# A two-layer retention and stick-breaking trunk: layers and retention loop written out, norm buffers moved to PSUM, and five smaller moves

## The reference

```python
for l in range(DEPTH):
    mod = c_act @ w_ada[l] + b_ada[l]
    shift1, scale1, gate1, shift2, scale2, gate2 = jnp.split(mod, N_MOD, axis=-1)
    h = _modulate(_rmsnorm(x, norm_mix_g[l]), shift1, scale1)
    x = x + gate1 * _mixer(h, w_in[l], w_ret_out[l], w_sb_out[l], w_mix_out[l])
    h2 = _modulate(_rmsnorm(x, norm_mlp_g[l]), shift2, scale2)
    u = jnp.square(jax.nn.relu(h2 @ w_up[l]))
    x = x + gate2 * (u @ w_down[l])
return _rmsnorm(x, final_g)
```

## Time and profile before

| | before |
|---|---|
| median of 3 runs | 2481.89 us (2480.94 to 2482.94) |
| the profiled execution: its time | 2484.95 us |
| its span | 2482.6 us |
| mean granted clock of TensorE | 0.98 |
| TensorE busy | 2403.6 us, 97% |
| GpSimd busy | 1126.0 us, 45% |
| VectorE busy | 1014.8 us, 41% |
| ScalarE busy | 893.6 us, 36% |
| read from HBM | 256.97 MB, 104 GB/s over the span |

### The profile page before, as it was taken

How to read it: one execution, slowest core, us unless ns; L and a number is a source line. 1 busy time by engine, 2 the same in 40 slices (tenths; PEclk the granted TensorE clock), 3 DMA queues, 4 the chain that set the end, 5 groups by cost and what they waited for, 6 DMA issues and landing times.

```text
span 2482.6 us, 33083 instructions
## 1 busy us (share of the span) xinstructions
PE 2403.6 (97%) x11946; PEld 1977.6 (80%) x11946; DVE 1014.8 (41%) x1521; ACT 893.6 (36%) x1005; POOL 1126.0 (45%) x1486
## 2 busy tenths in 40 slices
PE   6999999999999999999979999999999999999998
PEld 5787788788888878888858878878888787888886
DVE  6555455624442341221345564552444322321223
ACT  3222122245557332332322222222556753322332
POOL 2444434443334545554543444444433445455552
PEclk6999999999999999999989999999999999999999
DMA  6533536322222323323323534334222223233231
GB/s 221 166 125 101 174 102 191 119 69 67 68 68 69 99 71 102 101 84 102 102 99 102 191 119 158 120 105 136 68 68 68 68 76 95 84 102 94 92 102 51
DMA packets 252468, 260.67 MB, mean 105 GB/s; under 512 B 4144, under 2 KB 250048, under 8 KB 252352
## 3 DMA queue, kind: packets, MB, share of 16 engines
q1 hardware_dynamic: 250816, 255.92, 31.9%
q10 hardware_dynamic: 1536, 3.17, 0.5%
HBM read 256.97 MB, written 2.10 MB: 104 GB/s over the span
## 4 chain that ended last, share of the span: by engine, by line
PE 91%; DVE 4%; DMA 3%; issue 1%; ACT 1%; DVEq 0%; SPq 0%; ACTq 0%
PE proj L689 60%; PE proj L726 11%; PE proj L711 6%; PE att L827 4%; PE att L780 3%; DVE slab L950 2%; PE att L812 2%; PE att L765 1%; PE att L839 1%; DMA slab<-in_w_ada 1%; DMA work<-in_w_ada 1%; PE att L675 1%; PE proj L656 1%; DVE h_lo L1022 1%; PE att L789 1%
## 5 line engine op out<-in xcount | busy, mean ns | idle before, releaser
L362 POOL TENSOR_TENSOR w_lo<-w_raw,w_hi 128x256 fp32r<-128x256 f32 x1472 | 1123.8, 795 | 1319.8 <-ACT w_hi L401 1319.1
L401 ACT ACTIVATE w_hi<-w_raw 128x1024 fp32r<-128x1024 f32 x368 | 384.6, 1053 | 585.1 <-PE proj L689 449.6
L689 PE MATMUL proj<-h_hi,w_hi 128*128 128x512 f32 x1472 | 586.1, 398 | 8.7 <-DVE work L1048 8.7
L689 PE MATMUL proj<-h_hi,w_lo 128*128 128x512 f32 x1472 | 575.0, 391 | 0.0
L689 PE MATMUL proj<-h_lo,w_hi 128*128 128x512 f32 x1472 | 575.0, 391 | 0.0
L689 PEld LDWEIGHTS proj<-h_hi,w_hi 128*128 128x128 f32 x1472 | 277.7, 189 | 70.5 <-DVE work L1048 9.5
L689 PE MATMUL proj<-y_hi,w_hi 128*128 128x512 f32 x832 | 324.8, 390 | 7.7 <-DVE ya L1113 7.7
L689 PEld LDWEIGHTS proj<-h_lo,w_hi 128*128 128x128 f32 x1472 | 277.9, 189 | 59.4 <-issue 3.8
L689 PEld LDWEIGHTS proj<-h_hi,w_lo 128*128 128x128 f32 x1472 | 277.5, 189 | 58.9
L689 PE MATMUL proj<-y_hi,w_lo 128*128 128x512 f32 x832 | 324.4, 390 | 0.0
L689 PE MATMUL proj<-y_lo,w_hi 128*128 128x512 f32 x832 | 324.2, 390 | 0.0
(11 more groups left out here) (146 smaller groups left out, 2518.2 us busy)
## 6 DMA issues: line engine op xcount, KB each, us to landing
w_raw<-in_w_in SPq DMA_DIRECT2D x88, 1024.0 KB, 5.1
slab<-in_w_ada SPq DMA_DIRECT2D x48, 1024.0 KB, 8.4
w_raw<-in_w_up SPq DMA_DIRECT2D x32, 1024.0 KB, 5.5
w_raw<-in_w_down SPq DMA_DIRECT2D x32, 1024.0 KB, 4.9
w_raw<-in_w_ret_out SPq DMA_DIRECT2D x16, 1024.0 KB, 5.0
work<-in_w_ada SPq DMA_DIRECT2D x8, 1024.0 KB, 5.7
w_raw<-in_w_sb_out SPq DMA_DIRECT2D x8, 1024.0 KB, 4.9
w_raw<-in_w_mix_out SPq DMA_DIRECT2D x8, 1024.0 KB, 5.0
```

The source lines that it names most:

```text
L362: ins = pool.tensor_tensor(w_lo[:, s, ks, :], w_raw[:, s // 2, ks, P * (s % 2):P * (s % 2 + 1)], w_hi[:, s, ks, :], ALU.subtract)
L401: act.activation(w_hi[:, 2 * s + j, :, :], w_raw[:, s, :, P * j:P * (j + 1)], ACT.Copy).then_inc(hi_ready, 1)
L689: last = pe.matmul(proj[:, j, :], w[:, slot, k, :], a[:, k, :], start=k == 0 and n == 0, stop=k == KT - 1 and n == 2)
```

## The change

- Layers and the retention passes are written out by Python in all engines but GpSimd; the loops over stick-breaking groups and MLP quarters stay. In the second pass of a layer `whole_unit` takes the place of `first_unit` for unit 0.
- Third and fourth norm buffer lie in PSUM: bank 5 and banks 2 and 3 of `att`. `rope_t` and `rot` have other places in `work`.
- ScalarE asks for the rotary table at the head of the layer. In layer 1 the splits of unit 0 and of the first half of unit 1 are done under the last down projection of layer 0.
- The last split ahead of the MLP norm (the second half of the MLP's second unit) moves into that norm.
- The third batch of adaLN sums follows every second half of the output projection, not each of the first four. Batches two and three of layer 1's second pass are left out with their loads and turns (`has_ada`); nothing uses them.
- `scale_and_shift` for the MLP norm and for the next layer is done at the start of stick-breaking.
- The first group's q, k, v are stored straight in `sb_now`, and VectorE's copies for it are gone.

```diff
--- before.py
+++ after.py
@@ -53,6 +53,13 @@
 ADA_LOOP = 3 * ADA_BATCH
 assert ADA_LOOP * RET_LOOPS == ADA_UNITS and ADA_FIRST == 2 * ADA_BATCH
 ADA_CREDIT = 2
+
+
+def has_ada(layer, i, batch):
+
+    return layer < DEPTH - 1 or i < RET_LOOPS - 1 or batch == 0
+
...
@@ -155,16 +162,13 @@
...
-        at_layer = (part(6144, 2, SEQ), part(7168, SEQ), part(7680, SEQ), part(0, 2, SEQ))
-
-        at_mlp = (part(0, 2, SEQ), part(1024, SEQ), part(1536, SEQ), part(2048, 2, SEQ))
...
-        rope_t = part(7424, 2, SEQ)
-        rot = part(8448, SEQ)
+        rope_t = part(8192, 2, SEQ)
+        rot = part(7680, SEQ)
...
@@ -195,6 +199,9 @@
...
+
+        at_layer = (part(6144, 2, SEQ), part(7168, SEQ), att[:, 5, :], att[:, 2:4, :])
+        at_mlp = (part(0, 2, SEQ), part(1024, SEQ), att[:, 5, :], att[:, 2:4, :])
...
@@ -282,14 +289,14 @@
...
-            with sp.Fori(0, DEPTH) as layer:
+            for layer in range(DEPTH):
...
-                with sp.Fori(0, RET_LOOPS) as i:
+                for i in range(RET_LOOPS):
...
-                            for k in ([], [], [], [0, 1], [2], [3])[n]:
+                            for k in ([], [], [], [0, 1], [2], [3])[n] if has_ada(layer, i, j) else []:
                                 load_ada(layer, i, ADA_BATCH * j + k)
...
-                        for k in ([], [8, 9], [10], [11])[m]:
+                        for k in ([], [8, 9], [10], [11])[m] if has_ada(layer, i, 2) else []:
                             load_ada(layer, i, k)
...
@@ -412,7 +419,7 @@
...
-                    if between and k % 2:
-                        between(k // 2)
+                    if k in between:
+                        between[k]()
...
@@ -431,17 +438,19 @@
...
-            with own.loop(DEPTH, 38) as layer:
+            for layer in range(DEPTH):
                 first = layer * LAYER_PAIRS
 
 
-                for j in range(2):
-                    split_weights(first, 0, j)
-                norm_affine(2 * layer, at_layer, lambda j: split_weights(first, 1, j) if j < 2 else None)
-
                 act.dma_start(rope_t, rope).then_inc(rope_in, 16)
-
-                with own.loop(RET_LOOPS, 2) as i:
+                if layer == 0:
+                    for j in range(2):
+                        split_weights(first, 0, j)
+                    norm_affine(0, at_layer, {1: lambda: split_weights(first, 1, 0), 3: lambda: split_weights(first, 1, 1)})
+                else:
+                    norm_affine(2 * layer, at_layer, {1: lambda: split_weights(first, 1, 1)})
+
+                for i in range(RET_LOOPS):
...
@@ -490,16 +499,16 @@
...
+                def store_k(pair, unit, half, to=sb_next):
+                    store_feature(pair, unit, half, tile2(to, now_k)[:, half, :])
+
...
+                def store_v(pair, unit, to=sb_next):
...
-                        act.activation(blocks(sb_next, now_v)[:, 2 * half:2 * half + 2, :],
+                        act.activation(blocks(to, now_v)[:, 2 * half:2 * half + 2, :],
...
@@ -530,10 +539,10 @@
...
-                    store_k(first, SB_FIRST, half)
-                store_v(first, SB_FIRST + 1)
+                    store_k(first, SB_FIRST, half, sb_now)
+                store_v(first, SB_FIRST + 1, sb_now)
                 for half in range(2):
-                    store_q(first, SB_FIRST + 2, half)
+                    store_q(first, SB_FIRST + 2, half, sb_now)
...
@@ -588,10 +597,11 @@
...
                         products(first, MIX + m, half)
-                        split_weights(first, MIX + m + 2, half)
+                        if (m, half) != (3, 1):
+                            split_weights(first, MIX + m + 2, half)
                         added(first, MIX + m, half)
                         square(2 * layer + 1, 2 * m + half, at_mlp)
-                norm_affine(2 * layer + 1, at_mlp)
+                norm_affine(2 * layer + 1, at_mlp, {1: lambda: split_weights(first, MIX + 5, 1)})
...
@@ -608,7 +618,7 @@
...
                             products(pair, MLP + 4 + m, half)
-                            if not last or m < 2:
+                            if not last or m < 2 or (layer < DEPTH - 1 and (m, half) != (3, 1)):
                                 split_weights(pair, MLP + 4 + m + 2, half)
                             if last:
                                 added(pair, MLP + 4 + m, half)
@@ -740,17 +750,17 @@
...
-            with pe.Fori(0, DEPTH) as layer:
+            for layer in range(DEPTH):
                 first = layer * LAYER_PAIRS
                 mean_square(2 * layer, at_layer)
...
-                with pe.Fori(0, RET_LOOPS) as i:
+                for i in range(RET_LOOPS):
                     pair = first + RET_PAIRS * i
                     for h in range(2):
                         head = 4 * layer + 2 * i + h
                         u = 6 * h
-                        if h == 0:
+                        if h == i == 0:
                             first_unit(pair, u, h_hi, h_lo, normed_ready(2 * layer), BY_TILE)
                         else:
                             whole_unit(pair, u, h_hi, h_lo)
@@ -767,14 +777,16 @@
...
-                        turn_ada(layer, i, h)
+                        if has_ada(layer, i, h):
+                            turn_ada(layer, i, h)
...
-                                pe.wait_ge(ada_taken, 6 * layer + 3 * i + h + 1)
+                                if has_ada(layer, i, h):
+                                    pe.wait_ge(ada_taken, 6 * layer + 3 * i + h + 1)
...
@@ -797,7 +809,8 @@
...
-                    turn_ada(layer, i, 2)
+                    if has_ada(layer, i, 2):
+                        turn_ada(layer, i, 2)
...
@@ -1029,12 +1042,13 @@
...
-            with own.loop(DEPTH, 302) as layer:
+            for layer in range(DEPTH):
                 first = layer * LAYER_PAIRS
                 dve.sem_inc(ada_summed, ADA_CREDIT)
-                scale_and_shift(layer, 0)
+                if layer == 0:
+                    scale_and_shift(0, 0)
                 norm(2 * layer, at_layer)
-                with own.loop(RET_LOOPS, 42 + 7 * ADA_LOOP) as i:
+                for i in range(RET_LOOPS):
...
@@ -1054,7 +1068,7 @@
...
-                        for q in range(ADA_BATCH):
+                        for q in range(ADA_BATCH if has_ada(layer, i, h) else 0):
                             sum_ada(layer, i, ADA_BATCH * h + q)
...
@@ -1072,7 +1086,8 @@
...
-                        take_ada(layer, i, h)
+                        if has_ada(layer, i, h):
+                            take_ada(layer, i, h)
...
@@ -1111,9 +1126,10 @@
                             products(pair, 12 + m, half)
                             k = 2 * m + half
                             free(dve.tensor_tensor(ya[:, k, :], ya[:, k, :], proj[:, half, :], ALU.add), half)
-                            if k < ADA_BATCH:
-                                sum_ada(layer, i, 2 * ADA_BATCH + k)
-                    take_ada(layer, i, 2)
+                            if k % 2 == 0 and has_ada(layer, i, 2):
+                                sum_ada(layer, i, 2 * ADA_BATCH + k // 2)
+                    if has_ada(layer, i, 2):
+                        take_ada(layer, i, 2)
...
@@ -1154,8 +1170,13 @@
...
-                take_qk(first, SB_FIRST + 2)
-                take_v()
+                scale_and_shift(layer, 1)
+                if layer < DEPTH - 1:
+                    scale_and_shift(layer + 1, 0)
+                for half in range(2):
+                    taken(first, SB_FIRST + 2, half)
+                dve.sem_inc(qk_now, 1)
+                dve.sem_inc(v_now, 1)
...
@@ -1196,7 +1217,6 @@
                         else:
                             add_square(2 * layer + 1, k - 1, at_mlp)
                             add_to_x(first, SB_OUT + m, half, k, gates + KT * GATE1)
-                scale_and_shift(layer, 1)
                 norm(2 * layer + 1, at_mlp)
```

More of the change, by code:

```diff
@@ L413, in norm, with norm_affine @@
                 act.activation(rstd, rstd, ACT.Exp, scale=-0.5).then_inc(rstd_ready, 1)
-            def norm_affine(n, buffers, between=None):
+            def norm_affine(n, buffers, between):
                 norm(n, buffers)
@@ L491, in store_feature, with store_q @@
                     split_weights(pair, unit + 2, half)
-                def store_k(pair, unit, half):
-                    store_feature(pair, unit, half, tile2(sb_next, now_k)[:, half, :])
-                def store_q(pair, unit, half):
-                    store_feature(pair, unit, half, tile2(sb_next, now_q)[:, half, :], SB_DIM ** -0.5)
-                def store_v(pair, unit):
+                def store_k(pair, unit, half, to=sb_next):
+                    store_feature(pair, unit, half, tile2(to, now_k)[:, half, :])
+                def store_q(pair, unit, half, to=sb_next):
+                    store_feature(pair, unit, half, tile2(to, now_q)[:, half, :], SB_DIM ** -0.5)
+                def store_v(pair, unit, to=sb_next):
```

(2 more changed lines are left out.)

## The result

The changed kernel takes 2440.01 us, the median of 4 runs (2438.05 to 2440.74); the kernel before took 2481.41 us beside it (2479.4 to 2482.94). The ratio is 0.9834, with a 95% interval of 0.9818 to 0.9849: 41.4 us faster, where 44.7 was forecast. The profiled execution took 2440.74 us with a span of 2439.0 us, 43.6 less than the span before; the mean granted clock is 0.985, before 0.98.

What follows compares the result with a forecast made beforehand. TensorE, busy 97% of the span, was taken as the bound. Gains of 47.9 us, less 1.5 and 1.7, gave 44.7; 2484.95 minus that is 2440.3, as a median 2437 us, range 2428 to 2450.

Steps and rivals of the forecast that it cites:

- rotary table: Start of both layers: asking for the table ahead of the norm removes TensorE's waits and slow units behind; gain 14.3 us.
- norm at the layer boundary: Between layers: ScalarE's branch wait and weight splits go, so TensorE starts as at the MLP norm; gain 3.8 us.
- pace of the layers' first units: Units behind the layer norms: norm buffers in PSUM bring them to the MLP norm's pace; gain 5.9 us.
- loop branch: End of the first retention passes: written out, the branch wait and the slow unit behind it go; gain 8.6 us.
- the wait for the last sum: Output projection: the last sum follows the seventh half, so TensorE waits some 0.5 us in three passes; 1.5 us back.
- clock behind the turned sums: Behind the small matmuls that turn the sums: one clock fall in three passes, at the lowest price seen; 1.7 us back.
- PSUM writes: The five norms: writing their buffers into PSUM taken as 0, bounds 2 us less to 6 more.
- my first rival: The clock falls at the turned sums in all three passes: 3 to 7 us less gain, 2440 to 2444; chance 0.17.
- Sums every second half: Output projection: a free half behind each adaLN sum means no bank is late; gain 9.5 us.
- Instruction blocks: Rival: the longer written-out code starves TensorE, slower than before, 2499 us at 0.8 us per block; chance 0.02.
- next wait in retention: Rival: output projection weights or the table's transfer beside the first weights come late; price 5 to 10 us; chance 0.08.
- slow PSUM: Rival: PSUM writes in the norms cost 0.3 us more each; 7 to 13 us, thus 2444 to 2450; chance 0.12.

Runs made afterwards that it cites:

- Run 8: Changed kernel with the first group stored aside and copied into place by VectorE again: 2442.29 us, +2.3.
- run 12: Changed kernel with norm buffers in SBUF, layer 1's first splits at the norm and the rotary table asked for behind the norm, together: 2458.76 us, +18.8.
- run 1: Changed kernel with the rotary table asked for behind the norm again: 2446.57 us, +6.6.
- Run 2: Changed kernel with the norm's buffers in SBUF again: 2444.11 us, +4.1.
- run 7: Changed kernel with layer 1's first weights split at the norm again, norm buffers kept in PSUM: 2440.21 us, +0.2.
- run 3: Changed kernel with the third batch's sums behind each of the first four halves again, the left-out batches staying out: 2438.09 us, 1.9 less.
- run 5: Changed kernel with the third batch's four sums behind half units 0, 1, 3 and 5: 2433.46 us, -6.5.
- run 9: Changed kernel with only TensorE's two retention passes of layer 0 in a hardware loop again: 2441.59 us, +1.6.
- run 4: Changed kernel with the third batch's small matmuls moved behind the first half of the next unit: 2432.96 us, -7.0.
- run 11: Changed kernel with sums behind half units 0, 1, 3 and 5, plus 15 unread matmuls in the waits of three norms: 2430.32 us, -9.7.
- run 6: Changed kernel with all sums of layer 1's last pass kept: 2443.11 us, +3.1.

## Why the prediction was right

The time, 2440.0, lies in the range and 3 us above the forecast. The terms, each read from the two traces:

| term | forecast | measured |
|---|---|---|
| rotary table: waits 8.7, units 13.47 + 13.94 to 2 x 10.88 | 14.3 | 14.4 |
| norm at the layer boundary, 7.71 to 3.88 | 3.8 | 3.8 |
| pace of the layers' first units, 16.2 + 16.9 to 12.56 + 13.40 | 5.9 | 7.1 |
| loop branch: its waits | 3.9 | 3.9 |
| clock behind the first passes: 4.7 of before gone | 4.7 | 4.7 |
| sums: four bank waits and the clock behind the longest | 9.5 | 9.5 |
| the wait for the last sum | -1.5 | -2.1 |
| clock behind the turned sums | -1.7 | -5.1 |
| two turns left out | 3.4 | 3.4 |
| first group in place, 2 x (2.02 - 0.7) | 2.4 | 2.6 |
| PSUM writes | 0 | 0 |
| shorter waits ahead of L721 and L748 | none | 1.3 |
| sum | 44.7 | 43.5 |

The spans differ by 43.6 us, so in sum the table leaves nothing over, though it omits terms of half a us: the first units of the two MLP stages together take 0.5 us longer than before. The medians differ by 41.4, within what runs scatter. The closeness is in part luck. The losses at the turned sums were 4.0 us larger than forecast, and the pace and two terms that I had too small or not at all gave 2.7 back.

*Rotary table, boundary, first group.* Right in mechanism and size. Run 8's trace confirms the last by itself (2.02 us of wait again). Of the boundary's 3.8 us, run 12 puts back 1.7 with the splits and the buffers. Runs 1 and 12 add what the trace of before could not say: the table's 14.4 us stand in the trace only while the norm is slow. Beside a quick norm, undoing the edit costs 6.6 us of time and 8.1 at its place: waits of 3.80 and 2.43, and units of 12.6 and 10.98 instead of 10.88.

*Pace.* I put the gain in both layers down to the buffers in PSUM. Run 2 bears that out in layer 0, where the unit goes back to near 16 us. In layer 1 it is half the story: the buffers alone (run 7, 12.7 us) or the splits made beforehand alone (run 2, 14.0) each bring most of it, and only with both undone (run 12) is the unit at 16.7. The term was 1.2 us too small: I took 13.64 us of the MLP norm as the floor, but layer 0's unit took 12.56. How long the clock stays down after a wait of 3.9 us differs: the same unit reads 12.56 in the changed kernel and 13.97 in runs 3 and 5, which don't touch it. A single unit behind such a wait is known to 1.4 us and no better.

*PSUM writes.* The value 0 held, the upper bound of 6 us did not come near. The Trainium skill (VectorE: DVE Perf Modes, The TRN2 errata) would have a PSUM source cost VectorE 62 cycles more; the trace does not agree for these instructions, which take 744 to 756 ns with both operands in SBUF away from GpSimd's work (L1017, L1030 in run 2), or with one in PSUM.

*Clock behind the turned sums: the step that failed.* "I take one fall in three passes, at the lowest price seen" was too few: it fell in all three, at 1.7 us each, which is my first rival (2440 to 2444, chance 0.17). With three falls at 1.7 the same sum gives 41.3. The medians differ by 41.4 and the spans by 43.6, so the agreement with the first to 0.1 is chance. My reason, that 2.02 us of waiting had passed without a fall, looked at the wait alone; what counts here is a wait of 0.68 us with 1.68 us of small matmuls behind it.

*Sums every second half.* The forecast sized the gain correctly and put it down to the wrong edit. The longest bank wait with its unit, 4.3 us, stood in layer 1's last pass, where the sums are left out altogether. In the other three passes 5.2 us were gained and 7.2 paid at the last sum; run 3, which takes the edit back, is 1.9 faster by the median and 3.1 by the span. One half unit of room is all that was missing: runs 4 and 5 keep the free banks, lose the wait, and gain 7.0 and 6.5.

*Loop branch.* Its wait went, but of the clock's part, 4.7, some 3.4 came back behind the turned sums at the same two places; run 9 shows that TensorE's branch in layer 0 costs 2.5 us of wait and 1.1 in the unit behind it there, and no second fall. *Instruction blocks, next wait in retention, slow PSUM:* none of these rivals left a trace. TensorE's matmuls show no wait by issue at all.

## What to carry to other kernels

When sums move off one engine's late path, look at when the *last* of them ends: a wait of 0.7 us right ahead of a stretch of small matmuls cost 2.4 us where the clock fell behind it, and moving either by half a unit of work gave it all back. Price edits at one place together: a table that arrives late, a norm that contends with GpSimd and weight splits in between were worth 18.8 us together and 10.9 one by one. Where TensorE has to wait for a few us, check the unit behind it for its pace before blaming the wait alone; filling the wait with unread matmuls gained 1 us or so a place until VectorE's pace took over.

## What was not expected of the hardware

- The fall of TensorE's clock (from 2.4 to 1.2 GHz, seen as spacing of 0.43 instead of 0.23 us) behind the wait of 0.68 us and the small matmuls is not certain. Over the kernels that have this wait with a unit right behind it, it fell in 18 of 27 cases, in the changed kernel in 3 of 3. With the same small matmuls and no wait (runs 3, 4, 5, 11) it fell in none of 12. The wait of 0.7 us ahead of the first scores, with no small matmuls behind it, passed without a fall. So did a plain wait of 2.43 us (run 1), but not one of 2.48 (the kernel before) or of 3.80 (run 1). What decides within the 27 is left open. It is not the edits alone: in runs 6, 7 and 8 a fall is missing in layer 0's retention, ahead of anything that their edits touch, and the first layer's first matmul starts at 53.0 to 53.8 us instead of 53.1. Whether a fall comes and goes between executions of the same kernel, one trace of each can't tell, so the 1.6 us of a missing fall need be no effect of the edit.
- Contention between VectorE and GpSimd is seen on both sides and needs two SBUF operands: with one in PSUM, VectorE's 1.2 us become 0.75 and GpSimd's 9.20 us for eight split operations 5.65. The Trainium skill (GPSIMD Engine Reference, Specifications) names two SBUF inputs of VectorE as a case of contention; the trace agrees. It is not all or nothing here: 1.2 us against 0.75, and 9.20 against 5.65.
- ScalarE's second step of the root (L420) takes 582 ns from PSUM to PSUM; in the kernel before and in run 2 it took 629 in SBUF. With the shift (687 ns here, 722 in run 2) these make 0.08 of the 0.12 us by which TensorE starts earlier than in run 2 (3.88 us after the norm's sum, not 4.00).
- The two small rows of TensorE's waits that nothing was done to fell by 0.1 us a case once the waits were on constants instead of a loop's registers (3.4 to 2.8, 2.2 to 1.5 us). That the form of the wait does it was not tested by itself.
